# Attention output of a hybrid decoder: values held stationary in column halves, softmax factors transposed in the slot and applied by VectorE one slot later

## What is computed

```
def dsa_attention(...):      # group A: 6 heads of 64, top-128 selected keys
    ...
        logits = jnp.where((dist >= 0)[:, None], logits, -jnp.inf)
        p = jax.nn.softmax(logits, axis=-1).astype(v.dtype)
        return jnp.einsum('bhqk,bqkhd->bqhd', p, v_sel)
...
def memory_attention(...):   # group C: 4 heads of 64, 256 memory tokens
    logits = jnp.einsum('bthd,bmhd->bhtm', qh, kh).astype(jnp.float32) * HEAD_DIM ** -0.5
    p = jax.nn.softmax(logits, axis=-1).astype(vh.dtype)
    return jnp.einsum('bhtm,bmhd->bthd', p, vh).reshape(B, T, MEM_W)
...
for l in range(DEPTH):
    x = x + 0.5 * swiglu(rms_norm(x, ffn1_norm[l]), ...)
    ...
    x = x + jnp.concatenate([out_a, out_b, out_c], axis=-1) @ w_out[l]
    x = x + 0.5 * swiglu(rms_norm(x, ffn2_norm[l]), ...)
```

## Time and profile before

| what | value |
|---|---|
| median of 3 runs | 2151.27 us (2148.92 to 2152.72) |
| the profiled execution | 2148.25 us |
| its span, first to last instruction | 2146.4 us |
| its mean granted TensorE clock | 0.999 |
| TensorE matmul busy | 2123.1 us (99%) |
| VectorE busy | 1044.4 us (49%) |
| ScalarE busy | 758.5 us (35%) |
| attention slots of layer 0 | 611.6 to 699.3 us |

### The profile page before, as it was taken

How to read it: one execution, slowest core, us unless ns; L and a number is a source line. 1 busy time by engine, 2 the same in 40 slices (tenths; PEclk the granted TensorE clock), 3 DMA queues, 4 the chain that set the end, 5 groups by cost and what they waited for, 6 DMA issues and landing times.

```text
span 2146.4 us, 31599 instructions
## 1 busy us (share of the span) xinstructions
PE 2123.1 (99%) x13057; PEld 1718.4 (80%) x13057; DVE 1044.4 (49%) x1419; ACT 758.5 (35%) x1046; POOL 353.0 (16%) x293
## 2 busy tenths in 40 slices
PE   9999999999999999999999999999999999999999
PEld 7888888777777888888888888887777778888887
DVE  5343333688666643433333433337886655433322
ACT  5222222474445422222232222234743454222211
POOL 0111011105013411101111010111040135010000
PEclk9999999999999999999999999999999999999999
DMA  5222223221111232222222222232212102222232
GB/s 195 98 93 91 100 94 110 103 99 42 60 52 39 79 117 91 92 89 105 94 98 98 98 98 91 94 129 94 85 42 91 41 20 101 96 96 98 93 108 74
DMA packets 30643, 192.38 MB, mean 90 GB/s; under 512 B 3216, under 2 KB 5392, under 8 KB 11984
## 3 DMA queue, kind: packets, MB, share of 16 engines
q1 hardware_dynamic: 30160, 189.80, 24.9%
q10 hardware_dynamic: 384, 1.14, 0.1%
HBM read 188.70 MB, written 2.10 MB: 89 GB/s over the span
## 4 chain that ended last, share of the span: by engine, by line
PE 89%; DVE 6%; ACT 2%; issue 1%; DMA 0%; SPq 0%; POOL 0%; DVEq 0%; ACTq 0%
PE psum L895 27%; PE psum L897 26%; PE psum L896 26%; PE psum L1326 2%; PE psum L1026 1%; PE psum L1310 1%; DVE wl L1749 1%; PE psum L1198 1%; PE psum L1195 1%; DVE acc L1832 1%; PE psum L1294 1%; DVE XL L1764 1%; DVE gkT L1863 0%; DVE wrk L1847 0%; PE psum L1268 0%
## 5 line engine op out<-in xcount | busy, mean ns | idle before, releaser
L895 PE MATMUL psum<-XH,wh 128*128 128x512 f32 x1904 | 760.4, 399 | 3.8 <-DVE wl L1749 1.8
L897 PE MATMUL psum<-XH,wl 128*128 128x512 f32 x1904 | 742.4, 390 | 0.0
L896 PE MATMUL psum<-XL,wh 128*128 128x512 f32 x1904 | 742.2, 390 | 0.0
L895 PEld LDWEIGHTS psum<-XH,wh 128*128 128x128 f32 x1904 | 357.9, 188 | 91.8 <-issue 14.4
L897 PEld LDWEIGHTS psum<-XH,wl 128*128 128x128 f32 x1904 | 357.8, 188 | 75.7
L896 PEld LDWEIGHTS psum<-XL,wh 128*128 128x128 f32 x1904 | 358.1, 188 | 74.3 <-issue 4.3
L1757 DVE TENSOR_TENSOR wl<-raw,wh 128x2048 fp32r<-128x2048 f32 x88 | 201.7, 2292 | 159.4 <-ACT wh L1396 159.4
L895 PE MATMUL psum<-HH,wh 128*128 128x512 f32 x704 | 273.9, 389 | 0.0
L896 PE MATMUL psum<-HL,wh 128*128 128x512 f32 x704 | 273.9, 389 | 0.0
L897 PE MATMUL psum<-HH,wl 128*128 128x512 f32 x704 | 273.9, 389 | 0.0
L1391 ACT ACTIVATE wh<-raw 128x2048 fp32r<-128x2048 f32 (+1 forms) x84 | 157.2, 1872 | 301.1 <-PE psum L897 301.1
(11 more groups left out here) (250 smaller groups left out, 1970.3 us busy)
## 6 DMA issues: line engine op xcount, KB each, us to landing
raw<-weights SPq DMA_DIRECT2D x143, 1024.0 KB, 4.8
raw<-weights SPq DMA_DIRECT2D x32, 896.0 KB, 4.4
xT<-xt SPq DMA_DIRECT2D x4, 512.0 KB, 6.2
memT<-memt SPq DMA_DIRECT2D x2, 1024.0 KB, 4.9
out<-xT SPq DMA_DIRECT2D x8, 256.0 KB, 5.8
stripsA<-strip_table SPq DMA_DIRECT2D x2, 768.0 KB, 6.3
raw<-weights SPq DMA_DIRECT2D x2, 512.0 KB, 6.5
stripsB<-strip_table SPq DMA_DIRECT2D x2, 512.0 KB, 7.4
```

The source lines that it names most:

```text
L895: pe.matmul(out_ap, a_hi, b_hi, start=first, stop=False)
L896: pe.matmul(out_ap, a_hi, b_lo, start=False, stop=False)
L897: return pe.matmul(out_ap, a_lo, b_hi, start=False, stop=last)
```

## The change

- The value product swaps its operands (new line 1325): the 64 value columns of a head are stationary (128 keys x 64), `pT` moves (128 tokens), and the two heads of a pair write partitions 0 to 63 and 64 to 127 of `bank[3]`. The result is already transposed. The two heads alternate within each key tile; both `pT` must be there first.
- The softmax factors are now needed along the free dimension. In slot p+1 VectorE takes the reciprocal of the pair's two sums, each read 64 times, into a 128x128 tile of `rrec` (line 2055, in every slot, last of its `att` part); in slot p+3 TensorE transposes it into `bank[3]` ahead of the pair's logits (line 1300).
- In slot p+3, after everything else of its `att` part, ScalarE copies product and factors, 256 columns, from `bank[3]` to `oA` (line 1659).
- In slot p+4 VectorE multiplies the two halves into `oN` (line 2042, 128x128, after the slot's maxima). At the end of a phase ScalarE rounds `oN` to `XH` (line 1640) and VectorE takes `XL` from `oN` (line 2049), all in that slot. The transposes of `oA` and the two VectorE operations on whole phases are gone. `rrec`, `oA` and `oN` lie in memory that the recurrence has freed (`EGr`).

```diff
@@ TensorE, attention(slot)
-                        if 0 <= p < N_PAIRS and phase_end(p):
-                            b, ph, done = phase(2 * p)
-                            pe.wait_ge(S["o_ev"], done + 1)
-                            for c in range(3 if ph else 2):
-                                mm = pe.transpose(bank[3][:, c * P:(c + 1) * P], oA[:, c * P:(c + 1) * P],
-                                                  const("ident"))
-                            mm.then_inc(S["o_t"], 1)
...
+                        p = slot - 3
+                        if 0 <= p < N_PAIRS:
+                            b, j = job(2 * p)
+                            pe.wait_ge(S["jr_done"], of("jr_done", p + 1))
+                            if p:
+                                pe.wait_ge(S["jo_done"], of("jo_done", p))
+                            else:
+                                pe.wait_ge(S["os_read"], of("os_read", NB))
+                            pe.transpose(bank[3][:, WA:WA + P], rrec[:, p % 3, :], const("ident"))
...
-                                if j in (0, H_A) and n:
-                                    pe.wait_ge(S["o_lo"], phase(n)[2])
...
-                                for i in range(nt):
-                                    v = (dvN[:, i, at0:at0 + DH] if j < H_A else mvN[:, i, at0:at0 + DH])
-                                    mm = pe.matmul(bank[3][:, at0:at0 + DH], pT[n % 4][:, i * P:(i + 1) * P], v,
...
+                            pe.wait_ge(S["jp_even"], p + 1)
+                            pe.wait_ge(S["jp_odd"], p + 1)
...
+                            for i in range(nt):
+                                for e, r in enumerate(rows):
+                                    mm = pe.matmul(bank[3][r, at0:at0 + P],
+                                                   vals[:, i, at0 + DH * e:at0 + DH * (e + 1)],
+                                                   pT[(2 * p + e) % 4][:, i * P:(i + 1) * P],
@@ ScalarE, attention(slot)
-                            act.wait_ge(S["o_t"], done + 1)
+                            act.wait_ge(S["jx_done"], of("jx_done", p + 1))
...
+                                           oN[:, 0:c1 - c0, :], ACT.Copy).then_inc(S["o_hi"], 1)
...
+                        p = slot - 3
+                        if 0 <= p < N_PAIRS:
+                            b, j = job(2 * p)
+                            c = (j if j < H_A else j - H_A) // 2
+                            act.wait_ge(S["jv_done"], 2 * p + 2)
+                            if p > 1:
+                                act.wait_ge(S["jx_done"], of("jx_done", p - 1))
+                            act.activation(oA[:, p % 2], bank[3].rearrange("p (c t) -> p c t", t=P)[:, c::3 - c, :], ACT.Copy
+                                           ).then_inc(S["jo_done"], 1)
@@ VectorE, attention(slot)
-                            chain.step(dve.reciprocal(rrec[:, b % 2, j0:j0 + nh], rsum[:, b % 2, j0:j0 + nh]))
...
-                            dve.tensor_tensor(oA[:, 0:nh * DH].rearrange("p (h d) -> p h d", h=nh),
-                                              bank[3][:, 0:nh * DH].rearrange("p (h d) -> p h d", h=nh), r,
-                                              ALU.mult).then_inc(S["o_ev"], 1)
+                        p = slot - 4
+                        if 0 <= p < N_PAIRS:
...
+                            dve.wait_ge(S["jo_done"], of("jo_done", p + 1))
+                            dve.tensor_tensor(oN[:, c, :], oA[:, p % 2, 0, :], oA[:, p % 2, 1, :], ALU.mult
+                                              ).then_inc(S["jx_done"], 1)
...
+                            dve.tensor_tensor(XL[sl], oN[:, 0:c1 - c0, :], XH[sl].bitcast(F32), ALU.subtract
+                                              ).then_inc(S["o_lo"], 1)
+                        p = slot - 1
+                        if 0 <= p < N_PAIRS:
+                            b, j = job(2 * p)
+                            dve.wait_ge(S["je_done"], 2 * p + 2)
+                            dve.reciprocal(rrec[:, p % 3, :].rearrange("p (e d) -> p e d", e=2),
+                                           rsum[:, b % 2, j:j + 2].unsqueeze(2).to_broadcast([P, 2, DH])
+                                           ).then_inc(S["jr_done"], 1)
```

More of the change, by code:

```diff
@@ L367 @@
                   w_done=4, vp_ps=8, vn_done=8, s_ps=7, s_done=7, sd_done=6, o_ps=8, oc_done=4,
[L368 removed]
+                  os_ps=4, os_read=4, or_done=4, op_done=4, jr_done=N_PAIRS, jo_done=N_PAIRS, jx_done=N_PAIRS, og_done=4, gh_done=3, gl_done=3, cb_done=18, tap_done=9, pr_done=24, ex_done=16, hf_hi=3, hf_lo=3,
                   sm_t=1, sp_e=1, sp_b=1, g_ready=1)
@@ L524 @@
 jl_done jm_done je_done jtr_done jp_even jp_odd jv_done
-o_ev o_t o_hi o_lo
+o_hi o_lo
 """.split()
@@ L595, in hybrid_trunk @@
         rsum = sb("rsum", [P, 2, JOBS])
-        rrec = sb("rrec", [P, 2, JOBS])
+        sb("behind_rsum", [P, 2, JOBS])
         memr = sb("memr", [P, 2])
@@ L630, in hybrid_trunk @@
         kg = sb("kg", [P, NB, WB])
+        with ExitStack() as third:
+            rrec = sb("rrec", [P, 3, P], F32, third)
+            oA = sb("oA", [P, 2, 2, P], F32, third)
+            oN = sb("oN", [P, 3, P], F32, third)
         EGr = sb("EGr", [P, 3, T])
@@ L2001, in attention @@
                     def attention(slot):
-                        p = slot - 4
-                        if 0 <= p < N_PAIRS and phase_end(p):
-                            b, ph, done = phase(2 * p)
-                            c0, c1 = (0, 3) if ph else (6, 8)
-                            dve.wait_ge(S["o_hi"], done + 1)
-                            sl = (slice(None), slice(c0, c1), slice(b * P, (b + 1) * P))
-                            dve.tensor_tensor(XL[sl], bank[3][:, 0:P * (c1 - c0)].rearrange("p (c t) -> p c t", t=P),
-                                              XH[sl].bitcast(F32), ALU.subtract).then_inc(S["o_lo"], 1)
-                        p = slot - 3
-                        ends = 0 <= p < N_PAIRS and phase_end(p)
-                        if ends:
-                            b, ph, done = phase(2 * p)
-                            j0, nh = (0, H_A) if ph else (H_A, H_M)
-                            dve.wait_ge(S["je_done"], 2 * p + 2)
-                            chain.step(dve.reciprocal(rrec[:, b % 2, j0:j0 + nh], rsum[:, b % 2, j0:j0 + nh]))
-                            chain.join()
                         p = slot
```

32 lines of the change are left out of this document (13 added, 19 removed).

## The result

The changed kernel takes 2162.34 us (median of 8 runs, 2156.97 to 2167.9) against 2151.99 for the kernel before (8 runs, one of them, at 7495 us, far off): ratio 1.005, 95% interval 1.0037 to 1.0063. It is slower by 0.5%, 10.4 us, where I had forecast 5.8. The profiled execution took 2166.43 us, its span 2164.4 us.

The account below looks back on a forecast made before the run. TensorE, busy 99%, bounds the kernel, but VectorE would set slots 5 to 14. Per layer 1.35 + 4.7 - 4.0 + 0.85 = +2.9 us, +5.8 in both: 2157 us, own range 2153 to 2164, overall range 2140 to 2168.

Parts of the forecast that it names:

- the rival of the cheap reciprocal: VectorE's wide reciprocal takes 0.2 us instead of 0.95, so the kernel gets faster, 2138 us; chance 0.20.
- B: Slots 5 to 14 of a layer: VectorE's queue sets the stretch, 42.0 us for 37.3, +4.7.
- the signs that I had named: 128x128 reciprocal about 1.03 us; slots 5 to 14: VectorE busy 40 of 42, TensorE waiting 8; slots 15 to 22 shorter; clock dip.
- The reciprocal's price: VectorE's 128x128 reciprocal takes 1.03 us, of which 0.95 counts in the queue; bounds 0.2 and 1.2.
- The key tile: TensorE's value product takes 0.25 us a key tile instead of 0.445, saving 0.195.
- The rival of the serial halves: In the value product the output halves do not overlap, 0.56 us a key tile: 2174 us; chance 0.10.
- the product's term in B: VectorE's 128x128 multiplication in slots 5 to 14: 0.29 us, 0.22 until the next may start.
- C: Slots 15 to 23 of a layer: TensorE's shorter key tiles make them 4.0 us shorter.
- the handoffs: Slots 15 to 23: TensorE's waits for ScalarE's late copy of product and factors cost about 1.0 us at phase ends.
- The clock: TensorE idling in slots 5 to 14 costs half a fall of its clock, 0.85 us a layer; bounds 0 and 3.4.
- The rival of repeated falls: TensorE's clock falls twice a layer, +10.9 us in both layers, 2162 us; chance 0.12.
- A: Slots 1 to 4 of a layer: reciprocals and multiplication ahead of weight halves on VectorE, +1.35 us.

Follow-up runs that it names:

- Experiment 8: Kernel before with the wide 128x128 reciprocal added on VectorE in each of the 20 slots, its result unused: 2161.73 us.
- experiment 1: Changed kernel with the reciprocal taken of the pair's two sums only (128x2), widened by two TensorE matmuls in place of the transpose: 2156.24 us.
- experiment 6: Changed kernel with the loop over the two heads outside the loop over the key tiles in the value product: 2164.12 us.
- Experiment 3: Changed kernel with GpSimd's additions of bias and mask replaced by fills of the same buffer with zeros: 2153.86 us.
- experiment 4: Changed kernel with VectorE's product moved ahead of the slot's maxima: 2148.91 us.
- experiment 10: Changed kernel with the product ahead of the maxima and GpSimd's additions replaced by fills with zero: 2146.87 us.
- experiment 7: Changed kernel with ScalarE's rounding copy of `oN` to `XH` moved behind its two copies to `pT`: 2157.37 us.
- experiment 9: Changed kernel with 20 idle 128x128 transposes on TensorE in slot 14, ahead of its wait for VectorE's maxima: 2160.11 us.
- Experiment 11: Changed kernel with the 128x2 reciprocal widened by matmuls, the product ahead of the maxima, and the `pT` copies ahead of the `XH` rounding: 2140.43 us.
- experiment 5: Changed kernel with the 128x2 reciprocal widened by two matmuls and the product ahead of the maxima: 2143.38 us.

## Why the prediction was right, and where it was off

**The mechanism was right.** VectorE takes over as the bound of slots 5 to 14, and the wide reciprocal is what does it. Experiment 8 puts that one instruction into the old kernel and gets 10.3 us; the rival of the cheap reciprocal is dead at 0.94 us. The unlooked-for part is that taking it out of the changed kernel gives back only 6 (experiment 1), since something else then holds B.

Of the signs that I had named, VectorE's 40 busy us (39.85, of 43.5 where I had 42) and the dip of the clock near slot 14 came. TensorE's idle time in B came too, 7.7 us, but not for the reason named: maxima and exponentials hold it for 2.9 us there, `pT` for 3.4 and a weight half for 1.3. The 4 us less in slots 15 to 22 did not come.

**The reciprocal's price** (1.03, 0.95 in the queue): measured 0.94 and 0.86, which makes ten of them 0.9 us cheaper in B than in my sum. **The key tile** (0.25): 0.22 plus 0.15 once a product. The rival of the serial halves did not occur; head by head only the third and fourth key tile would cost more (experiment 6). All products of a layer together take 13.1 us (46 x 0.22 + 20 x 0.15), where 0.25 a key tile made 11.5.

**The step that failed is the product's term in B, "0.29 us, 0.22 until the next may start".** It came from a row where GpSimd stood still, and it sits in the one place in the slot where GpSimd has just been released. Eight products a layer make the 20 of them 5.0 us longer than 20 x 0.28, half of it in B. Experiment 3 takes the overlap away and gets 8.5 us back, nearly the whole time by which the changed kernel is slower. B is then +3.9, where I had +4.7, and the cheaper reciprocal accounts for that difference. The miss was thus larger than the 4.6 us between 10.4 and 5.8: without the contention the kernel is 1.7 us slower than the one before beside it, 4.1 us under my +5.8. That +5.8 came as near to +10.4 as it did is in part luck, since these two errors, 8.5 missing and the rest 4.1 too high, stand against each other.

**C was to be -4.0 and is -1.0.** TensorE's own saving of 5.0 is real: with the product first C is 36.5, 5.15 shorter than before (experiment 4). Of the missing 4.2, some 2.2 go with the low clock (below) and some 2.0 with the handoffs, for which I charged 1.0. Four rows of the changed kernel's timelines, on VectorE, ScalarE and TensorE, show the chain that they form at an end of a phase (here still in B):

```profile
671.36 0.83 DVE L2042 TENSOR_TENSOR oN<-oA 128x128 f32<-128x128 f32 x1
...
672.23 0.52 ACT L1640 ACTIVATE XH<-oN 128x384 fp32r<-128x384 f32 x1 [3.78 <-DVE oN L2042]
672.66 0.64 ACT L1650 ACTIVATE pT<-psum 128x256 f32<-128x256 f32 x2
...
673.17 1.09 PE L1289 MATMUL psum<-cst,at 128*128 128x128 f32 x4 [0.98 <-ACT pT L1650]
```

ScalarE has nothing to do for 3.78 us, and the copies to `pT`, for which TensorE waits, stand behind a rounding that waits for the product, which waits behind two maxima. I had noted that ScalarE's copies stand behind the rounding, but priced only `jo_done`, at 1.0; the waits for `pT` alone are 5.0 us a layer. Between experiments 3 and 10 the product's place is worth 2.4 to 2.5 us a layer in C, the clock included, and 3.0 to 3.7 in B; experiment 7 moves the wait from `pT` to `oA` and recovers 2.4 a layer of the slots. This is the second error, and it could have been found by following `oN` through ScalarE's queue instead of stopping at VectorE's.

**The clock** (0.85 a layer): the clock lost in the slots is 5.1 and 6.8 us, against 1.7 and none before. What it costs depends on the stretch. In B it can cost nothing, where VectorE's queue covers it: experiment 4 has 39.04 us with none lost and 39.02 with 1.7, and experiment 9 takes 1.9 us of it out of layer 0 and leaves B at 43.5. It need not be so: in experiment 8 B is 1.6 us longer with 1.7 lost. In C it costs about what it takes: in experiments 1, 3, 6 and 10 the C of the two layers differs by 0.9 us for each us by which the clock lost in them differs (in 7 and 9 by 0.6, in the changed kernel by 1.1). The changed kernel loses 2.6 and 2.4 us in its C, which at 0.9 makes 2.3 and 2.1 us. So this term was low by some 1.4 us a layer. The fall is itself a consequence of the waits at the end of B, and which of them brings it was not tried one by one.

The rival of repeated falls named 2162 us, the measured time, and its condition was met: I had asked for two falls a layer, 3.4 us of clock, and B and C lose 5.1. Its number fits by luck all the same. It charged every us lost in full, B's too, and left out the contention, without which the time is 2153.9 us with 3.4 us of clock still lost in B and C of each layer (experiment 3).

**A** (+1.35): mean of both layers +0.5. A low clock of 1.7 us falls into it in layer 0 before and in layer 1 after, and makes it 1.5 to 1.6 longer; at like clock A is 0.6 longer without it (18.97 to 19.55) and 0.45 with it.

In sum, by the experiments, one at a time from the changed kernel: contention 8.5, the wide reciprocal 6, the product's place 13 (with about half of the contention, by the lengths of the products). They overlap and do not add up to 10.4, against which stands TensorE's saving of about 10 in both layers. Experiment 11 keeps that saving but for the widening matmuls; the products that are still stretched in it lie mostly where TensorE sets the pace.

## What to carry to other kernels

A vector instruction that is moved to a spot right behind the one that releases GpSimd must be priced with GpSimd running beside it, not by a row where it was alone: the same product took 0.28 us and 1.17 us. And try an instruction whose result another engine rounds or copies at the head of its queue, which gave 13.4 us here; follow it to the last engine that stands behind it before calling the handoff a microsecond. Take a reciprocal of the few numbers that there are, and widen it elsewhere: that gave 6 us here, though the widening took some of C.

## What the runs showed of the hardware that I had not expected

- VectorE's product of two SBUF operands, 0.28 us alone, lasts until 0.15 us after the end of the GpSimd addition of two SBUF operands that started before it (up to 1.18 us); beside a GpSimd fill it keeps its 0.29 us. In the trace it is a long instruction, not a wait.
- RECIPROCAL takes 0.155 us for 2 elements a partition (experiment 1) and 0.94 for 128: 6.2 ns an element.
- Matmuls of 64 weight and 128 moving columns that alternate between the halves of the output take 0.22 us a key tile, four records. The Trainium skill, TensorE: Matmul & The Clock Gate (Part 3), lets a weight load overlap only with another row group; these share theirs and still run at this rate, so the trace does not agree. Head by head the rate holds for two key tiles and falls from the third on (1.51 us for four, against 1.02): by the starts in experiment 6, a record ran beside one of the other half up to four records ahead of its turn. Why four is open.
- Clock lost costs C about 0.9 us for each us lost, since TensorE sets the pace there, and B nothing in experiment 4 and in layer 0 of experiment 9, while in experiment 8 B is 1.6 us longer with 1.7 lost.
- A matmul takes a stationary operand that repeats one column 64 times, and so widens a column for TensorE: two of them take 0.27 to 0.37 us where one transpose took 0.20, and C is 1.4 us longer a layer (experiments 4 and 5).
